# Products with the values in front of the turns of the probabilities, in a two-layer attention trunk on one core

## The reference

```python
def banded_attention(q, k, v, max_dist, sink=None):
    ...
    s = jnp.einsum('bnqgrd,bnkgd->bngrqk', qb, kb).astype(jnp.float32) * SCALE
    ...
    s = jnp.where(mask, s, MASK_VALUE)
    m = jnp.max(s, axis=-1, keepdims=True)
    ...
    p = jnp.where(mask, jnp.exp(s - m), 0.0)
    den = jnp.sum(p, axis=-1, keepdims=True)
    ...
    o = jnp.einsum('bngrqk,bnkgd->bnqgrd', (p / den).astype(v.dtype), vb).reshape(B, S, H, Dh)

def reference(...):
    ...
    for i in range(DEPTH):
        norm, mixer, w_out = layers[i % N_MIXERS]
        x = x + mixer(rms_norm(x, norm)) @ w_out
    return rms_norm(x, final_norm)
```

## Time and profile before

| | |
|---|---|
| median of 3 runs | 1343.69 us (1342.52 to 1344.02) |
| profiled execution, its own time | 1343.39 us |
| its span | 1341.6 us |
| mean granted TensorE clock | 0.990 of full speed |
| TensorE busy | 1280.9 us |
| VectorE busy | 774.4 us |
| ScalarE busy | 637.9 us |

### The profile page before, as it was taken

How to read it: one execution, slowest core, us unless ns; L and a number is a source line. 1 busy time by engine, 2 the same in 40 slices (tenths; PEclk the granted TensorE clock), 3 DMA queues, 4 the chain that set the end, 5 groups by cost and what they waited for, 6 DMA issues and landing times.

```text
span 1341.6 us, 24576 instructions
## 1 busy us (share of the span) xinstructions
PE 1280.9 (95%) x8714; PEld 1190.6 (89%) x8714; DVE 774.4 (58%) x2337; ACT 637.9 (48%) x1767; POOL 403.5 (30%) x443
## 2 busy tenths in 40 slices
PE   5999999999899999999999999999999999988896
PEld 4998998987699999899989999899999899976896
DVE  5744453546572545566556765557666467666825
ACT  6444462545641445555546554455545465545111
POOL 2312051240341121211305722208722138323410
PEclk9999999999999999999999999999999999989998
DMA  5101022122455201101112311213210222133623
GB/s 197 40 17 48 25 64 71 33 79 59 134 169 183 95 24 52 38 25 26 49 48 66 81 56 35 64 36 87 91 31 21 83 58 74 56 94 84 188 95 126
DMA packets 101079, 97.29 MB, mean 73 GB/s; under 512 B 30688, under 2 KB 87520, under 8 KB 100960
## 3 DMA queue, kind: packets, MB, share of 16 engines
q1 hardware_dynamic: 100960, 95.73, 24.0%
HBM read 79.46 MB, written 16.25 MB: 71 GB/s over the span
## 4 chain that ended last, share of the span: by engine, by line
PE 85%; DVE 5%; ACT 2%; POOL 2%; DMA 2%; issue 2%; SPq 1%; DVEq 0%; POOLq 0%; ACTq 0%
PE j_bank L1152 59%; PE o_bank L1291 7%; PE t_bank L1270 6%; PE s_bank L1257 5%; PE j_bank L1235 3%; PE s_bank L1259 2%; DVE ht_lo L1779 1%; PE s_bank L1152 1%; DMA w_raw<-in_w_out 1%; PE o_bank L1152 1%; DMA gate<-in_positions 1%; ACT probs L1384 1%; POOL rot L1041 1%; DVE xr L1769 0%; POOL qk L1044 0%
## 5 line engine op out<-in xcount | busy, mean ns | idle before, releaser
L1152 PE MATMUL j_bank<-w_hi,ht_hi 128*128 128x384 f32 (+1 forms) x1328 | 451.5, 340 | 17.4 <-DVE ht_lo L1779 8.9
L1152 PE MATMUL j_bank<-w_hi,ht_lo 128*128 128x384 f32 (+1 forms) x1328 | 439.7, 331 | 0.0
L1152 PE MATMUL j_bank<-w_lo,ht_hi 128*128 128x384 f32 (+1 forms) x1328 | 439.7, 331 | 0.0
L1018 POOL TENSOR_TENSOR w_lo<-w_raw,w_hi 128x768 fp32r<-128x768 f32 (+1 forms) x60 | 107.9, 1799 | 596.7 <-ACT w_hi L1375 595.4
L1152 PEld LDWEIGHTS j_bank<-w_hi,ht_hi 128*128 128x128 f32 x1328 | 252.7, 190 | 29.2 <-issue 25.5
L1152 PEld LDWEIGHTS j_bank<-w_lo,ht_hi 128*128 128x128 f32 x1328 | 253.0, 190 | 0.0
L1152 PEld LDWEIGHTS j_bank<-w_hi,ht_lo 128*128 128x128 f32 x1328 | 252.7, 190 | 0.0
L1384 ACT ACTIVATE probs<-probs,stat 128x256 f32<-128x256 f32 (+1 forms) x512 | 231.0, 453 | 43.9 <-DVE stat L1621 41.9
L767 ACT COPY probs_t<-t_bank 128x256 f32<-128x256 f32 (+1 forms) x128 | 57.9, 452 | 297.1 <-PE o_bank L1291 291.6
L1375 ACT ACTIVATE w_hi<-w_raw 128x768 fp32r<-128x768 f32 (+1 forms) x120 | 88.1, 763 | 84.4 <-PE j_bank L1152 48.3
L1613 DVE CUSTOM_DVE_ANT_0 probs<-s_bank,masks 128x256 f32<-128x256 f32 x224 | 86.2, 421 | 58.1 <-PE t_bank L1270 57.4
(11 more groups left out here) (169 smaller groups left out, 1834.5 us busy)
## 6 DMA issues: line engine op xcount, KB each, us to landing
w_raw<-in_w_qkv SPq DMA_DIRECT2D x64, 384.0 KB, 3.3
coef<-coef_dram SPq DMA_DIRECT2D x96, 128.0 KB, 3.0
w_raw<-in_w_gate SPq DMA_DIRECT2D x32, 256.0 KB, 3.4
mix_dram<-xr SPq DMA_DIRECT2D x12, 512.0 KB, 3.5
w_raw<-in_w_out SPq DMA_DIRECT2D x16, 384.0 KB, 3.6
qk<-mix_dram SPq DMA_DIRECT2D x12, 512.0 KB, 4.3
xr<-in_x SPq DMA_DIRECT2D x8, 512.0 KB, 7.3
out<-xr SPq DMA_DIRECT2D x8, 512.0 KB, 2.7
```

The source lines that it names most:

```text
L1018: pool.tensor_tensor(quarter(n, q, 1), raw_quarter(n, q), quarter(n, q, 0).bitcast(F32), ALU.subtract).then_inc(w_lo_done["p"], 1)
L1152: last = pe.matmul(to, a(x_, kt), b(y_, kt), start=(start and kt == kts[0] and x_ == y_), stop=(stop and kt == kts[-1] and x_ == 1))
```

## The change

In every pair TensorE takes the products with the values right behind the scores, and the turns behind them. At the end of a layer it takes the products of units 12 and 13 first, then the turns of 14 and 15, then their products. Nothing else is changed: the same instructions, the same semaphores and counts, the same order on all other engines.

```diff
@@ -1322,12 +1322,12 @@
                         pair = (a, a + 1)
                         for slot in pair:
                             score(s, slot)
+                        for b, u in [unit_before(s, slot, V_BACK) for slot in pair]:
+                            if b:
+                                times_v(b, u)
                         for b, u in [unit_before(s, slot, TURN_BACK) for slot in pair]:
                             if b:
                                 turn(b, u)
-                        for b, u in [unit_before(s, slot, V_BACK) for slot in pair]:
-                            if b:
-                                times_v(b, u)
                         for item in pair_work(s, a):
                             if item[0] == "fill":
                                 fill(*item[1:])
@@ -1340,9 +1340,11 @@
                         if a == UNITS - 2 and s.last:
                             early_rows(layer, 0, EARLY_ORDER[:FRONT_ROWS])
                 last = steps[-1]
+                for u in range(UNITS - V_BACK, UNITS - TURN_BACK):
+                    times_v(last, u)
                 for u in range(UNITS - TURN_BACK, UNITS):
                     turn(last, u)
-                for u in range(UNITS - V_BACK, UNITS):
+                for u in range(UNITS - TURN_BACK, UNITS):
                     times_v(last, u)
                 early_rows(layer, 0, EARLY_ORDER[FRONT_ROWS:])
                 early_rows(layer, 1, EARLY_ORDER[:FRONT_ROWS])
```

## The result

The changed kernel takes 1352.58 us (median of 4 runs, 1349.64 to 1354.81), the kernel before beside it 1343.54 us (4 runs, 1342.52 to 1344.02): ratio 1.006, 95% interval 1.0047 to 1.0072. It is slower by 0.6%, where 1340.8 us, a little faster, was forecast, and it lies outside the range given. The profiled execution has a span of 1353.0 us, 11.4 more than before; it is the slowest of the four. Lines behind 1343 have moved down by two (VectorE's masks are L1611 and L1615, the bias L1623, ScalarE's exponentials L1386, the weight splits L1377 and L1582, its copy of a gate piece L1404).

The account below looks back on a forecast made before the run. The kernel was taken as bound by TensorE, busy 95% of the span, plus its few waits. Terms of -2.5, -0.8 and +0.4 us summed to -2.9, giving 1340.8 us from a median of 1343.7, range 1337.0 to 1346.0.

Parts of the forecast that it names:

- part 2: VectorE's masks start 0.7 to 1.1 us later; slack covers most pairs, waits elsewhere net 0.8 us gained, 1 us either way.
- slack of 3.2 us: Ordinary pair: second bias done at 592.24, next scores at 595.40, set against 0.9 us of lateness.
- 10.5 us in 18 waits: TensorE's waits counted over 128 pairs: scores for bias, turns for exponentials, products and coefficient turns for a copy.
- Part 1: TensorE's steps between kinds of instruction: 52 pairs whose work begins with a piece each 0.05 us shorter, 2.5 us gained.
- The three steps: Start to start in an ordinary six-turn pair: scores to products 0.81, products to turns 0.80, turns to third piece matmul 1.08.
- the forecast was +0.3: Pair with turns at 529.76: scores wait longer but the wait for exponentials falls away, next piece's third matmul 0.3 us later.
- -1.1: Turn at 553.30 that waited 1.48 us for exponentials: products fill the wait, next fill 1.1 us earlier.
- the wait at 783.63: Another TensorE wait, whose mask is held by other work, not by a turn: estimated 0.5 us gained.
- Part 3: Layer ends: products of unit 14 start some 0.2 us later behind their turn's copy, +0.2 us, twice.
- B: Rival, chance 0.10: late masks make next scores wait for the bias, in some pairs with pieces too; slower, 1347.5 us.
- A: Rival, chance 0.19: the steps between kinds gain nothing, leaving 1343.3 us.
- C: Rival, chance 0.08: the step from scores to products is dear, 0.14 us, giving 1345.8 us.

Follow-up runs that it names:

- Experiment 6: Changed kernel with the old order (turns first) only in pair 10 of steps 6, 9 and 12: 1347.34 us, ratio 1.0023 to the kernel before.
- Experiment 8: Changed kernel with SyncE's loads of raw weights issued ahead of the store of the values in the same slot: 1347.73 us, ratio 1.0021.
- Experiment 7: Changed kernel with the old order only in pair 14 of steps 7, 10, 13 and pair 0 of steps 8, 11, 14: 1351.86 us, ratio 1.0058.
- experiment 2: Kernel before, old order, each even unit's mask also waiting for the products of the unit three before: 1363.96 us, ratio 1.0147.
- experiment 5: Changed kernel with a third buffer of probabilities, two-byte masks and small tiles sharing places, whole output: 1336.58 us, ratio 0.9937 to the kernel before.
- experiment 12: Kernel before, old order, with a third buffer of probabilities and two-byte masks, whole output: 1343.42 us, ratio 0.9991.
- experiment 1: Kernel before with only the new order at the two layer ends, old order inside the pairs: 1344.26 us, ratio 0.9999.

## Why the prediction was wrong

**What failed: one sentence of part 2.** "The copies and the emptying of banks that stand behind the masks on VectorE are late by as much, and catch up where VectorE waits for the piece of its own pair anyway." I looked for the lateness at the bias, for which the next scores wait, and there was slack of 3.2 us. But behind a late mask stand, in program order, VectorE's weight split and emptying, behind the late exponentials ScalarE's weight split, and from these hang GpSimd's split and rotation and SyncE's queue. These don't lead back to TensorE in the same pair but one to three pairs later, and there was no slack: the kernel before already waited 0.7 us in three places for the gate copy and 2.4 us in five for the rotation. The prediction named the lateness, and took the path by which it comes back at nothing; its list of "10.5 us in 18 waits" leaves these two rows out. Step 6 in the timeline of the kernel before, between pair 10 and the gate pieces:

```profile
661.51 1.14 ACT L1375 ACTIVATE w_hi<-w_raw 128x512 fp32r<-128x512 f32 x2
...
662.18 0.69 DVE L1580 TENSOR_TENSOR w_lo<-w_raw,w_hi 128x512 fp32r<-128x512 f32 x1
...
662.73 1.28 POOL L1018 TENSOR_TENSOR w_lo<-w_raw,w_hi 128x512 fp32r<-128x512 f32 x1 [16.71 <-ACT w_hi L1375]
...
663.43 0.22 DVE L1640 COPY v<-j_bank 128x64 f32<-128x64 f32 x1
...
663.72 0.37 SPq L852 DMA_DIRECT2D v_dram<-v  x1
...
664.13 1.13 SPq L782 DMA_DIRECT2D w_raw<-in_w_qkv  x2
...
668.00 0.84 ACT L1375 ACTIVATE w_hi<-w_raw 128x768 fp32r<-128x768 f32 x1 [0.99 <-DMA w_raw<-in_w_qkv]
...
670.10 0.60 ACT L1402 ACTIVATE gate<-j_bank 128x512 f32<-128x512 f32 x1
...
670.75 0.50 PE L1152 MATMUL j_bank<-ht_hi,w_hi 128*128 128x512 f32 x1 [0.25 <-ACT gate L1402]
```

The same place in the timeline of the changed kernel:

```profile
662.66 1.14 ACT L1377 ACTIVATE w_hi<-w_raw 128x512 fp32r<-128x512 f32 x2
...
663.88 1.28 POOL L1018 TENSOR_TENSOR w_lo<-w_raw,w_hi 128x512 fp32r<-128x512 f32 x1 [16.59 <-ACT w_hi L1377]
...
664.07 1.64 DVE L1582 TENSOR_TENSOR w_lo<-w_raw,w_hi 128x512 fp32r<-128x512 f32 x1
...
666.17 0.21 DVE L1642 COPY v<-j_bank 128x64 f32<-128x64 f32 x1
...
666.45 0.37 SPq L852 DMA_DIRECT2D v_dram<-v  x1
...
666.86 1.13 SPq L782 DMA_DIRECT2D w_raw<-in_w_qkv  x2
...
670.90 0.85 ACT L1377 ACTIVATE w_hi<-w_raw 128x768 fp32r<-128x768 f32 x1 [1.36 <-DMA w_raw<-in_w_qkv]
...
672.89 0.58 ACT L1404 ACTIVATE gate<-j_bank 128x512 f32<-128x512 f32 x1
...
673.52 0.50 PE L1152 MATMUL j_bank<-ht_hi,w_hi 128*128 128x512 f32 x1 [1.83 <-ACT gate L1404]
```

TensorE itself runs 1.18 us later here (scores at 662.70 and 663.88). ScalarE's split is late by 1.15, no more than that. VectorE's split is late by 1.89 and takes 1.64 us instead of 0.69, because it now falls beside GpSimd's; so the store goes 2.73 later, and with it the next raw weights, which stand behind it on SyncE's queue though VectorE's split had freed their buffer 1.15 us before. ScalarE splits them in front of its copy of the gate piece, and the next gate piece waits for that copy. A lateness of about 1 us thus becomes 1.89 at the start of VectorE's split and 2.84 at its end, and is then carried nearly unchanged (2.73 to 2.90) to the gate copy; TensorE, 1.18 late when it starts the pair, is 2.77 late at the next gate piece.

Experiment 6 takes away its beginning (VectorE's split stands at 662.57, ahead of GpSimd's, and takes 0.69 again). Experiment 8 takes out a link in the middle: its trace keeps the slow split and breaks the chain behind it.

```profile
663.26 1.64 DVE L1582 TENSOR_TENSOR w_lo<-w_raw,w_hi 128x512 fp32r<-128x512 f32 x1
...
664.93 0.82 SPq L782 DMA_DIRECT2D w_raw<-in_w_qkv  x2
...
665.84 0.38 SPq L852 DMA_DIRECT2D v_dram<-v  x1
...
668.64 1.67 ACT L1377 ACTIVATE w_hi<-w_raw 128x768 fp32r<-128x768 f32 x2
...
670.40 0.60 ACT L1404 ACTIVATE gate<-j_bank 128x512 f32<-128x512 f32 x1
```

The second chain, to the fills behind a group's end, begins on ScalarE: in the changed kernel its split behind the exponentials is late, GpSimd's split waits for that, and the rotation stands behind GpSimd's split. The timeline of the kernel before, step 8:

```profile
747.37 1.82 POOL L1018 TENSOR_TENSOR w_lo<-w_raw,w_hi 128x768 fp32r<-128x768 f32 x1 [1.36 <-ACT w_hi L1375]
...
749.15 1.10 POOL L1041 TENSOR_TENSOR rot<-qk,sines 128x96 f32<-128x96 f32 x1
...
754.44 0.63 PE L1235 MATMUL j_bank<-ident,qk 128*128 128x128 f32 x4 [0.32 <-POOLq L1049]
```

and of the changed kernel:

```profile
751.11 2.27 POOL L1018 TENSOR_TENSOR w_lo<-w_raw,w_hi 128x768 fp32r<-128x768 f32 x1 [2.76 <-ACT w_hi L1377]
...
753.34 0.38 POOL L1041 TENSOR_TENSOR rot<-qk,sines 128x96 f32<-128x96 f32 x1
...
757.88 0.63 PE L1235 MATMUL j_bank<-ident,qk 128*128 128x128 f32 x4 [0.94 <-POOLq L1049]
```

GpSimd starts 3.74 us later where TensorE is 2.8 later, and the fill, which waits for the last step of the rotation (L1049), runs 3.44 later. Experiment 7 shows this chain in its trace, but not in the time of whole runs. At pair 12 of step 2 VectorE's split is slow as well (1.36 us instead of 0.69), but I did not take the small losses at pair 12 of steps 1 and 2 apart; experiment 2 has losses there too (+0.72, +0.25).

**Part 1, right in kind, half in size.** The three steps read 0.81, 0.80 and 1.08, and the idle of the weight load at L1270 is 21.9 us, as forecast (21). At the piece's first loads it fell by 4.7 us, where 9 had been forecast, and at L1291, where it was to stay, it fell from 22.7 to 18.7. The 98 pairs with small changes gained 1.12 us, and the 113 such pairs of experiment 5 against experiment 12 gained 1.3, where I had 2.5. I measured the gain at the third matmul of the piece. In pairs of six turns all of it lasts until the next scores (0.05 each). In pairs of eight turns the piece's first matmuls behind the turns come some 0.03 further apart, and 0.02 is left. By the Trainium skill (TensorEngine Tiling (Array Packing), Key Properties), each change of tiling mode drains TensorE; the traces agree that every border has a price before and after, and show that the price depends on what stands behind it.

**Part 2, the pairs without a piece.** At the earlier trace rows the forecast was +0.3, and it is +0.40 (0.96 lost, 0.56 regained in the next pair); at the earlier trace rows -1.1, and it is -1.16 (0.54 lost, 1.70 regained); the wait at 783.63 of the earlier trace rows gave -0.57 for -0.5. All such places together gave -0.3 for -0.8, within the 1 us allowed, though the sum holds what the clock did in step 15. These are the places that I had worked through in the timeline, one by one; the others I had covered with one sentence.

**Part 3.** Expected +0.4, nothing measurable in experiment 1.

**The rivals.** B had the right sign and the right cause (later masks, in pairs where a DMA already holds an engine), but it looked for the wait at the scores. The bias waits grew by 3.4 us; the gate and fill waits, which it doesn't name, carry most of the rest. With 1347.5 us it was too small, and its chance of 0.10 too low. A and C are refuted by the start-to-start times.

## What to carry to other kernels

An edit that delays one engine's input by 1 us delays everything behind it in that engine's program, so the cover has to be counted for each of these (splits, emptyings, the queues that wait for them) up to where it comes back to the bottleneck, pairs later, and not only for the tile on which the edit acts. Where a reordering is sound and a buffer's release spoils it, a further buffer can turn it round: here from +0.6% to -0.6%, while the same buffer with the old order gave nothing. And a load whose buffer is free shouldn't stand in a queue behind a store that waits for compute; here it cost nothing until something got late, and then 5 us. A list of the bottleneck's waits is read to its last row: the small waits that exist already show where there is no slack.

## What the runs showed of the hardware

- VectorE's split of 128x512 takes 0.69 us in the 7 places of the kernel before where GpSimd computes nothing meanwhile, and as much in the 8 where GpSimd's instruction begins after it. In the 5 where one of GpSimd's was already running it took 0.93 to 1.78 us, and each time it ended 0.54 or 0.55 after that one's end. (Over the 13 places with GpSimd beside it, the mean is 0.94 before and 1.18 after.) In step 6 of the changed kernel it took 1.64: it began 0.19 us after GpSimd's split and ended 0.55 after that one's end. The Trainium skill (SBUF — State Buffer, Terms) says that the two share a pair of ports which one holds for a whole instruction while the other is blocked; by that rule VectorE would do its 0.69 us from 665.16 on and end at 665.85 (an estimate); the trace agrees but for 0.14 us, with 665.71. Which of the two begins first is thus a matter of an edit that touches neither.
- A wait of TensorE can cost twice. In experiment 7 the gate piece of step 9 waited 2.25 us, and for the 3 us behind the wait the granted clock was 0.50, the lower of the two levels (1.2 of 2.4 GHz):

```profile
859.00:862.00 3.00, 0.74 (x4) 0.49 (x3) 0.96 (x1) 2.36 (x5) 1.05 (x1) 0.99 0.37 76
862.00:865.00 3.00, 3.00 (x8) 2.32 (x7) 1.38 (x2) 0.44 (x1) 0.77 (x1) 0.50 0.59 189
```

(Columns: window, its length, busy time with instructions of PE, PEld, VectorE, ScalarE, GpSimd, the granted clock, the DMA share, GB/s.) The pair lost 3.62 us there. In the changed kernel's own profile the same place waited 1.53 us, the clock stayed at 1.00, and 1.27 was lost. Experiment 7's runs spread more (1344.9 to 1356.6) than those of the kernel before beside them (1341.7 to 1348.4), and the spread goes with the clock: the mean granted clock was 0.991 in the fastest and 0.983 to 0.984 in the three slowest, and 0.008 of 1350 us are 11 us. That such waits bring the lower level about was not tested by itself.
- The clock moves the layer ends by more than the change did: in the 30 us from 410 on the granted clock was 0.94 in the profiled execution of the kernel before and 1.00 in that of experiment 1, which was 1.62 us shorter at this end; 0.06 of 30 us are 1.8.
